# Forty column tiles of w_in as seven block products per pair

## The reference, cut

```
h = rms_norm(x, norm_mix_pre)                                  # x is (1, 512, 2048) float32
proj = h @ w_in + b_in                                         # w_in (2048, 11272)
hg_q, hg_f, hg_i, hg_g, ml_qk, ml_v, ml_o, ig, fg, gate_a, gate_b = split(proj)
y_a = hgrn2_mix(hg_q, hg_f, hg_i, hg_g)                        # chunked gated recurrence, 8 heads of 128
q, k = split(silu(causal_conv4(ml_qk)))
y_b = mlstm_mix(q, k, ml_v, ml_o, ig, fg)                      # chunked matrix memory, 4 heads
merged = sigmoid(gate_a) * (y_a @ w_up_a) + sigmoid(gate_b) * (y_b @ w_up_b)
x = x + rms_norm(merged @ w_out, norm_mix_post)
h = rms_norm(x, norm_ffn_pre)
gate = causal_conv3(h @ ffn_w_gate);  up = h @ ffn_w_up        # 2048 x 5632 each
x = x + rms_norm((gelu(gate) * up) @ ffn_w_down, norm_ffn_post)
```

## Time and profile before

| | |
|---|---|
| median of the runs | 2806.91 us (2806.22 to 2807.24) |
| profiled execution, first to last instruction | 2804.6 us |
| TensorE busy | 2770.7 us, 99% |
| VectorE, ScalarE, GpSimd busy | 1670.6, 1218.3, 350.0 us |
| granted TensorE clock | 0.998 of full speed |

### The profile page before, as it was taken

The page is one execution under the profiler, slowest core; times in us unless marked ns, Lnnn a source line. Parts: engine busy times, 40 slices in busy tenths (PEclk is TensorE's granted clock), DMA queues, the critical chain, the costliest instruction groups (busy, mean ns, idle before and its releaser), DMA issues.

```text
span 2804.6 us, 37979 instructions
## 1 busy us (share of the span) xinstructions
PE 2770.7 (99%) x13971; PEld 2337.5 (83%) x13971; DVE 1670.6 (60%) x1864; ACT 1218.3 (43%) x1462; POOL 350.0 (12%) x420
## 2 busy tenths in 40 slices
PE   8999999999999999999989999999999999999998
PEld 7888888888888888888868888888888888888887
DVE  5232344344333234442668787788788878878788
ACT  4242443432222222222465555555555555555554
POOL 1000000000000000000000122222222222222213
PEclk9999999999999999999999999999999999999999
DMA  4323334332332334434534788887888888888876
GB/s 175 97 83 113 97 98 117 93 97 92 103 94 83 106 93 141 157 136 146 201 133 144 181 165 166 186 167 161 189 170 164 180 179 162 170 184 163 164 177 240
DMA packets 451446, 404.48 MB, mean 144 GB/s; under 512 B 13075, under 2 KB 357271, under 8 KB 448553
## 3 DMA queue, kind: packets, MB, share of 16 engines
q1 hardware_dynamic: 397672, 294.69, 34.7%
q0 software_dynamic: 49088, 100.33, 21.7%
q10 hardware_dynamic: 4608, 8.39, 0.8%
HBM read 302.69 MB, written 100.66 MB: 144 GB/s over the span
## 4 chain that ended last, share of the span: by engine, by line
PE 97%; DVE 1%; ACT 1%; issue 0%; DMA 0%; POOL 0%; SPq 0%; DVEq 0%; POOLq 0%; ACTq 0%
PE ps L1002 20%; PE ps L625 17%; PE ps L1006 10%; PE ps L628 8%; PE ps L914 6%; PE ps L1039 5%; PE ps L1040 5%; PE ps L1041 5%; PE ps L667 4%; PE ps L669 4%; PE ps L668 4%; PE ps L643 1%; PE ps L637 1%; PE ps L646 1%; PE ps L705 1%
## 5 line engine op out<-in xcount | busy, mean ns | idle before, releaser
L1766 DVE TENSOR_TENSOR w_lo<-raw,w_hi 128x2048 fp32r<-128x2048 f32 x126 | 288.8, 2292 | 481.9 <-ACT w_hi L1146 481.8
L1722 POOL DMA_DIRECT2D down_sums<-arena x304 | 262.3, 968 | 905.4 <-ACT arena L1479 881.3
L1146 ACT CAST w_hi<-raw 128x2048 fp32r<-128x2048 f32 x127 | 242.1, 1907 | 237.7 <-PE ps L669 176.3
L2192 DVE TENSOR_TENSOR sum_ring<-quads 128x1024 f32<-128x1024 f32 x165 | 202.2, 1225 | 170.7 <-PE ps L1006 137.4
L1435 ACT CAST op_ring<-sum_ring 128x1024 fp32r<-128x1024 f32 x165 | 173.8, 1053 | 270.9 <-DVE sum_ring L2192 270.9
L1002 PE MATMUL ps<-hl,op_ring 128*128 128x512 f32 x1064 | 266.0, 392 | 2.7 <-ACT hl L1413 1.6
L625 PE MATMUL ps<-h_hi,w_hi 128*128 128x512 f32 x1024 | 245.1, 392 | 0.0
L628 PE MATMUL ps<-h_hi,w_lo 128*128 128x512 f32 x1024 | 242.5, 389 | 0.0
L625 PE MATMUL ps<-h_lo,w_hi 128*128 128x512 f32 x1024 | 242.5, 389 | 0.0
L1002 PEld LDWEIGHTS ps<-hl,op_ring 128*128 128x128 f32 x1064 | 193.2, 189 | 39.2 <-ACT hl L1413 2.0
L628 PEld LDWEIGHTS ps<-h_hi,w_lo 128*128 128x128 f32 x1024 | 192.2, 188 | 39.9
(11 more groups left out here) (363 smaller groups left out, 4753.3 us busy)
## 6 DMA issues: line engine op xcount, KB each, us to landing
raw<-in_w_in SPq DMA_DIRECT2D x88, 1024.0 KB, 5.2
down_sums<-arena POOLq DMA_DIRECT2D x320, 256.0 KB, 6.6
quads<-in_ffn_w_gate SPq DMA_DIRECT2D x88, 512.0 KB, 4.7
quads<-in_ffn_w_up SPq DMA_DIRECT2D x88, 512.0 KB, 4.7
quads<-in_ffn_w_down SPq DMA_DIRECT2D x88, 512.0 KB, 7.9
raw<-in_w_out SPq DMA_DIRECT2D x24, 1024.0 KB, 5.1
merge_gates<-arena ACTq DMA_DIRECT2D x32, 256.0 KB, 2.0
raw<-in_w_up_a SPq DMA_DIRECT2D x8, 1024.0 KB, 5.6
```

The costliest lines, as they stand in the source:

```text
L1146: act.copy(w_hi[:, s, :], raw[:, s, :]).then_inc(hi_ready, 1)
L1722: pool.dma_start(dst, src, accum_op=ALU.add).then_inc(acc_added[s], 16)
L1766: dve.tensor_tensor(w_lo[:, s, :], raw[:, s, :], f32(w_hi[:, s, :]), ALU.subtract).then_inc(lo_ready, 1)
L2192: dve.tensor_tensor(sum_of(i, pos), quads[:, a, :], quads[:, b, :], ALU.subtract if q in (M7, M6) else ALU.add).then_inc(ff_sum, 1)
```

## The change

The 40 column tiles of F, Q, G, QK and O become 20 pairs of block products, in one stage right after I: `Fori` over 5 groups of 4 pairs, 7 products a pair. It is the form with seven products and fifteen additions: four sums of weight quads, four sums of h that are made once, and additions of the products. Some of these happen in PSUM (P2 onto P1's bank, P7 onto P6's, P3 onto P5's, after ScalarE has copied what stood there). Of the rest VectorE makes those that read PSUM, and the folds of two half banks; GpSimd makes the two whose inputs are both in SBUF (P6 + P1, and P5 + P1P6P7).

Four more moving operands t_ops (T1 to T4) are made in the I stage; P1, P2 and P3 read h itself, hi and lo being two parts of one tensor now. ScalarE applies bias and function to each finished tile and stores it to DRAM from its own queue (256 KB each). v_hg goes to DRAM too, from GpSimd's queue, since the arena holds T1 to T4. f_all, q_all and v_hg (2 MB each) are read back on SP's queue when the last pair's products free their places; the G, QK and O tiles come back one by one on GpSimd's queue, where they are used.

The 32 gate tiles are spread anew: 2 after the products (LEAD), 3 in each HGRN2 round (ROUND), 2 after them (MID) with four gatings each, 3 in each mLSTM round, 4 at the end with two gatings each. The convolution and SiLU of the 8 QK tiles move into the V stage, one behind each unit's lo part and row step, and the SiLU ahead of ScalarE's next hi part. The order within the HGRN2 round changes: the next round's log, scans and exponentials are made earlier in the round. The V bias is loaded by GpSimd behind y_lo of the last HGRN2 gating, the first two QK tiles and the store of gate tile 15. Semaphores of the FFN are shared with the new stage by offsets.

```
+LEAD, ROUND, MID = 2, 3, 2
+P1, P4, P2, P6, P5, P7, P3 = range(7)
...
+            def load_in_quads(r):                       # SP
+                c = GROUP_COLUMNS[r // GROUP_PAIRS] + 2 * P * (r % GROUP_PAIRS)
+                for part, n, k, sums, lo in ((A22, 1, 1, 1, P4), (A11, 0, 0, 3, P1), (A21, 1, 0, 3, None), (A12, 0, 1, 4, P2)):
+                    if r:
+                        sp.wait_ge(weights_summed, 4 * (r - 1) + sums)
+                        if lo is not None:
+                            sp.wait_ge(op_lo_ready, 7 * (r - 1) + lo + 1)
...
-            cm_phase(U_F, N_F, NU_F)
-            cm_phase(U_Q, N_Q, NU_Q)
+            IN_BANK = {P1: 0, P2: 0, P6: 1, P7: 1, P5: 2, P3: 2, P4: 3}
+            IN_MOVING = {P1: lambda j: h_both[:, :, j, 0:TH], P2: lambda j: h_both[:, :, HALF + j, 0:TH],
+                         P3: lambda j: h_both[:, :, HALF + j, TH:T], P5: lambda j: t_ops[T1][:, j, :, :],
...
+            def in_product(i, k, q):                    # TensorE
...
+                elif q in (P2, P7, P3):
+                    pe.wait_ge(product_copied, 4 * r + {P2: 1, P7: 3, P3: 4}[q])
+                pe.wait_ge(op_hi_ready, o + 1)
+                for j in range(HALF):
+                    pe.matmul(ps[:, bank, :], w[0][:, j, :], IN_MOVING[q](j), start=(j == 0 and q in (P1, P4, P6, P5)), stop=False,
...
+            def in_hi_part(o):                          # ScalarE
+                r, q, slot = o // 7, o % 7, IN_SLOT[o % 4]
+                if o >= 4:
+                    act.wait_ge(op_done, o - 3)
...
+            for r in range(IN_PAIRS):                   # GpSimd
+                p1 = in_p1[:, r % 2, :]
+                pool.wait_ge(product_copied, 4 * r + 3)
+                pool.tensor_tensor(in_p6, in_p6, p1, ALU.add).then_inc(pool_added, 1)
+                pool.wait_ge(product_copied, 4 * r + 4)
+                pool.wait_ge(product_added, 3 * r + 1)
+                pool.tensor_tensor(in_p5, in_p5, p1, ALU.add).then_inc(pool_added, 1)
...
+            split_lo(*un_i(0, 4))                       # VectorE, I stage
+            dve.tensor_tensor(second[T1], first[T2], first[T1], ALU.subtract).then_inc(h_summed, 1)
+            dve.wait_ge(h_summed, 1)
+            dve.tensor_tensor(second[T2], first[T3], second[T1], ALU.subtract).then_inc(h_summed, 1)
+            dve.tensor_tensor(second[T3], first[T3], first[T2], ALU.subtract).then_inc(h_summed, 1)
             dve.wait_ge(vbias_loaded, 16)
-            v_block(0, U_I, v_hg, vbias_hg, 0, q0=2)
+            for n in range(TT):
+                i_tile(0, n)
...
+            def in_interval(r, k):                      # VectorE
+                o, now, before = 7 * r + k + 2, r < IN_PAIRS, r > 0
+                if now and k in (2, 3):
+                    in_sum_of(r, k + 1)
+                if k in (5, 6) and r + 1 < IN_PAIRS:
+                    in_sum_of(r + 1, k - 4)
+                if o < IN_OPS:
+                    in_lo_part(o)
+                if k == 0 and before:
+                    in_c12(r - 1)
...
             dve.wait_ge(vbias_loaded, 32)               # VectorE, V stage
-            v_block(0, U_V, v_ml, vbias_ml, 2, rows_step)
+            def first_block(q):
+                rows_step(q)
+                qk_conv_tile(q)
+            v_block(0, U_V, v_ml, vbias_ml, 2, first_block)
```

More of the change, by code:

```diff
@@ L164, in build @@
             _, neg_ident = at("gap2", 16), at("neg_ident", 0.5)
+        with ExitStack() as over:
+            t_ops = [over.enter_context(nc.sbuf_tensor(f"t{k}", [P, HALF, 2, TH], F32R)) for k in (1, 2, 3, 4)]
         ctx.enter_context(nc.sbuf_tensor("arena_keep", [P, ARENA], F32))
@@ L647, in unit_goes_on, with gate_unit @@
                 last.then_inc(unit_done, 1)
[L649 to L652, removed]
+            def gate_unit(m):
+                cm_unit(gate_u(m), m, m % 2)
             def of_h(part, j, n):
@@ new lines, in block_of_h @@
+            def block_of_h(k, t, to):
+                rows, tok = slice(HALF * k, HALF * k + HALF), slice(TH * t, TH * t + TH)
+                then(dve.tensor_tensor(to, f32(h_hi[:, rows, tok]), f32(h_lo[:, rows, tok]), ALU.add))
+            split_lo(*un_i(0, 3))
+            dve.wait_ge(h_lo_ready, 4 + 16)
+            first, second = ([t[:, :, r, :] for t in t_raw] for r in range(2))
+            block_of_h(0, 0, first[T1])
+            block_of_h(0, 1, first[T2])
+            block_of_h(1, 1, first[T3])
@@ new lines, in _ @@
+            dve.wait_ge(prm_turned, 1)
+            block_of_h(1, 0, first[T4])
+            dve.wait_ge(h_summed, 2)
+            dve.tensor_tensor(second[T4], first[T4], second[T2], ALU.subtract).then_inc(h_summed, 1)
+            split_lo(*un_i(1, 2))
+            parameters(1)
+            for k, t in enumerate((T2, T4, T1, T3)):
+                dve.wait_ge(h_op_hi, k + 1)
+                dve.tensor_tensor(t_ops[t][:, :, 1, :], second[t], f32(t_ops[t][:, :, 0, :]), ALU.subtract).then_inc(h_op_lo, 1)
@@ L1893, in chunks @@
+            split_gate(1)
             def chunks(t):
@@ new lines, in _ @@
+            for m in range(M_MID, M_ML):
+                split_next(m)
+                if m == M_MID:
+                    dve.wait_ge(hg_out_kept, TT + 1)
+                for h in range(4 * (m - M_MID), 4 * (m - M_MID) + 4):
+                    gating(h, q_all[:, h, :], 0, PHG, ya_hi, ya_lo, 0)
+                if m == M_MID:
+                    dve.wait_ge(act_step, 2)
+                    dve.tensor_tensor(wg_lo, wg_raw, f32(wg_hi), ALU.subtract).then_inc(wg_split, 1)
+            for s in range(2):
+                then(dve.memset(qk_pre[s][:, 0:3], 0.0))
@@ L2224, in plus_m5 @@
-                dve.wait_ge(ff_op, done(i, p, M5))
-                dve.tensor_tensor(ff_x[:, X3, :], ff_x[:, X3, :], ps[:, bank, :], ALU.add).then_inc(ff_part, 1)
+                dve.wait_ge(product_copied, IN_SUMS + 3 * pair + (2 if first else 3))
+                dve.wait_ge(op_done, done(i, p, M5))
+                dve.tensor_tensor(ff_x[:, X3, :], ff_x[:, X3, :], ps[:, bank, :], ALU.add).then_inc(product_added, 1)
             def m1_minus_m5(i, p, bank):
-                dve.wait_ge(ff_part, 6 * (PAIRS * i + p) + 3)
```

848 lines of the change are left out of this document (541 added, 307 removed).

## The result

| | before | after |
|---|---|---|
| median of the runs | 2806.7 us (4 runs, 2806.22 to 2807.24) | 2772.01 us (4 runs, 2770.21 to 2772.95) |
| ratio | | 0.9876, 95% interval 0.9862 to 0.989 |
| profiled span | 2804.6 us | 2770.4 us |
| TensorE, VectorE, ScalarE, GpSimd busy | 2770.7, 1670.6, 1218.3, 350.0 us | 2731.2, 1946.9, 1326.9, 434.9 us |

What follows compares the result with a forecast made beforehand. TensorE was taken as the bound, busy 2770.7 of 2804.6 us. Terms of -44.9, +1.0 and +8.3 summed to -35.6 us, a span of 2769.0; plus 2.3 gave 2771, stated as 2772, range 2763 to 2789.

Steps and rivals of the forecast that it cites:

- Term 1: Product stage: 40 column tiles (435.2 us) become 140 block products of 2.7875 us (390.3 us), net -44.9 us.
- Term 2: Product stage: side-engine work fits beside the products, VectorE at 18.9 of 19.5 us a pair; 0 us booked.
- rival B: Product stage: VectorE becomes the bound, each GpSimd addition costing it 2.0 us; 16 to 24 us lost, 2788 to 2796; chance 0.10.
- rival D: Product stage: pairs paced above the products, slower than before; decides at 1.8 us a pair, 21.3 instead of 19.5; chance 0.03.
- Term 3: I stage: making the four moving operands delays the evacuation of tile 0; +1 us.
- Term 4: Rounds of three gate tiles instead of four: thin margins but everything covered, 0 us.
- 4.0 of 4.5 us: HGRN2 round: ScalarE's evacuation with table load (2.9 us) and two copies (1.1 us) fit within transposes and opening matmuls.
- Rival C: Joints: eight rounds each 1 to 2 us late through a table load, read-back 5 late; 2785 to 2791; chance 0.12.
- Term 5: V stage, now sharing gating and QK convolution: TensorE waits 2.3 us at unit 2, 5.9 before the second block; 8.3 us altogether.
- just in time: V stage, units 3 and 4: the chain to the next low part takes 10.8 us against 10.88, so no wait there.
- The sum: Whole kernel: -35.6 us on the profiled span of 2804.6, so 2769.0; with 2.3 us to the median 2771, stated as 2772.
- Rival A: V stage: no waits there, the sum being the products' gain alone; 2762 to 2765 us; chance 0.12.

Runs made afterwards that it cites:

- experiment 3: Kernel after the change, with GpSimd's two additions of a pair made by VectorE and GpSimd idle in the product stage: 2770.99 us.
- experiment 4: Kernel after the change, with one low part of each pair (that of P6) made twice by VectorE: 2771.93 us.
- experiment 5: Kernel after the change, with three low parts of each pair (P2, P5, P1) made twice by VectorE: 2809.02 us.
- experiment 7: Kernel after the change, with ScalarE copying the turned outputs three times instead of once in each HGRN2 round: 2776.45 us.
- experiment 8: Kernel after the change, reordered in stages I and V (evacuations, convolution before row step, exponential and logarithm, V bias wait): 2762.81 us.
- experiment 2: Kernel after the change, with only unit 4's convolution moved behind the evacuation in stage V's first block, row step still ahead: 2768.23 us.
- experiment 1: Kernel after the change, with stage V's first-block evacuation right behind unit 4's low part, row step and convolution afterwards: 2767.06 us.
- experiment 6: Kernel after the change, with GpSimd's two additions on VectorE and three low parts of a pair made twice: 2799.25 us.

## Why the prediction was right, and where it was off

**Term 1** was -44.9 us, and is -44.2 (435.2 less 391.03): a product takes 2.793 us and not 2.7875. The operand in two places costs nothing, as chosen.

**Term 2**, nothing, is right. The VectorE figure is off, above all by what was named under rival B and left out: records of neighbours overlap by 0.08 us. The durations of the 353 records in the stage sum to 365.3 us where the busy time is 342.9, 1.1 us a pair. So its busy time is 17.15 us a pair, not 18.9, 88% and not 97%. GpSimd's part in it was taken as 1.7 us; it is 1.6 in the pair shown (0.50 + 1.10) and 1.4 over the stage (experiment 3: 39 additions of 0.6 us are 23.4 us more work, and yet VectorE is 4.6 us less busy; 28 us in 20 pairs). Experiments 4 and 5 put the edge between 1.2 and 3.7 us more VectorE work a pair. **Rival B** falls with this: it priced the two additions at 4.0 us a pair. So does **rival D**'s pace, though its point of decision holds: at 1.85 us a pair in the median the time is that of the kernel before, for the 1.8 predicted.

The rule of the Trainium skill (SBUF — State Buffer, Who interferes with whom) that the engine that issues second fully blocks is borne out by the meetings at 305 and 317 us; so is its exception, the addition that reads PSUM. By that rule alone the prediction had priced 2 x 1.33 us; the rows give 1.6 us. At most what is left of the other's instruction is lost, and by these records 0.1 to 0.3 us less: 0.72 of 0.98 us by the addition at 305.18, 0.50 of 0.63 by the low part behind it, 1.10 of 1.23 by the folds.

**Term 3**, 1.0 us: 0.69 of idle time, and the first product starts 0.95 us later than the first tile of the kernel before (109.53 for 108.58). **Term 4**, 0: right, with more room than given. The step that put a table load behind the tile's end, "4.0 of 4.5 us", is wrong for the kernel after: the load lies in ScalarE's idle time, and about 2.3 us are used (experiment 7). **Rival C** had counted on that load. For the kernel before the reading was right; there the load came when the tile was done:

```profile
348.27 1.28 ACT L1230 ACT_TABLE_LOAD   x1 [6.14 <-PE ps L646]
```

**Term 5**, 8.3 us: 8.5 (the stage's matmuls take 96.36 us from the first start to the last, 87.89 in the kernel before), but not by its parts. Unit 1 0.22 (0.1), unit 2 1.88 (2.3), both near. The second block waits 3.98 and not 5.9: "just in time" for unit 4 was too careful, its low part is ready 1.5 us ahead of the turn, a convolution takes 2.9 us from start to start, not 3.2, and the row step 1.8, not 1.9; 5.9 - 1.5 - 0.3 - 0.1 = 4.0. What filled the sum again was not foreseen: the slow clock after the wait, 1.7 us, and 0.7 us around the three waits that their idle times don't hold. That the errors cancel is luck.

**The sum** gave 2769.0 us for the span, which is 2770.4: 0.7 us more in term 1, 0.2 in term 5, 0.5 behind the start of the up-projections. The 2.3 us from the span to the time came from the span of one execution and the median of others; within one execution of the kernel after it is 1.6 us (2771.98 less 2770.4). So the agreement to the microsecond is luck, too: the errors of 1.4 us and 0.7 us nearly cancel, and the sum's own figure was 2771.

**Rival A** is what experiment 8 reached, by edits to the order alone; its 2762 to 2765 us hold.

What stays open: why the wait of 1.9 us at unit 2 is followed by the low clock in experiments 2 and 3 and not in the kernel after or in experiments 1, 4, 5 and 6; and why ScalarE's table load comes ahead of its wait in the kernel after and behind it in the kernel before. The wait at unit 1, which the V bias ends, is anything from 0.22 to 1.33 us in the kernel after and experiments 1 to 6, whose order is the same up to there; so no cause is read from differences of 1 us between them.

## What to carry to other kernels

When a stage with much spare time on the side engines is shortened on TensorE, the gain is the plain difference in matmuls as long as the fullest side engine keeps some free time (here VectorE could still be busy 94% of the stage, in experiment 4, without a wait of TensorE); take that free time from idle rows that TensorE ends, and subtract the overlap of neighbours before adding up. The loss is in the joints: work that lost its own stage lands ahead of an evacuation, and moving the evacuation in front of it gives it back. Here an addition on GpSimd with both inputs in SBUF relieved VectorE of nothing, because VectorE worked on two SBUF inputs beside it: 1.4 us a pair lost for 1.2 saved.

## What the runs showed of the hardware, unexpectedly

A wait of TensorE can cost more than its length. At each of the waits of 3.9 to 4.2 us in stage V (at unit 1 in experiment 7, ahead of the second block in the kernel after and in experiments 4, 5, 6 and 7) the granted clock fell to 0.50, during the wait or within 1 us of its end, and stayed there for 3 to 7 us, 1.5 to 2.3 us lost; after a wait of 1.9 us it was so in experiments 2 and 3 and not in the kernel after and experiments 1, 4, 5 and 6, and after one of 2.34 us in experiment 3 it was not. Such stretches stand outside stage V as well, behind several shorter waits: in the kernel before at 1467 to 1471 us, in the kernel after at 1399 to 1406. Experiment 8 has none up to the FFN.
